# The norms' factors by Sqrt on ScalarE and reciprocal on VectorE, in a two-block transformer kernel on one core

## The reference

```
def rmsnorm(x, g):
    xf = x.astype(jnp.float32)
    y = xf * lax.rsqrt(jnp.mean(xf * xf, axis=-1, keepdims=True) + EPS)
    return (y * g.astype(jnp.float32)).astype(x.dtype)

# a layer of the first stack
h = modulate(x, g_pre_mix[l], sh_m, sc_m)          # rmsnorm(x, g) * (1 + scale) + shift
x = x + gt_m * rmsnorm(mixer(h), g_post_mix[l])
h = modulate(x, g_pre_ffn[l], sh_f, sc_f)
x = x + gt_f * rmsnorm(swiglu(h), g_post_ffn[l])

# a layer of the second stack
x = x + mixer_2(rmsnorm_2(x, norm_mix))
x = x + swiglu_2(rmsnorm_2(x, norm_ffn), w_gate, w_up, w_down)
```

## Time and profile before

| | |
|---|---|
| median of 3 runs | 3402.07 us (3381.19 to 3405.97) |
| the profiled execution | 3400.29 us, of it the span 3398.5 us |
| TensorE busy | 3115.9 us, 92% of the span |
| VectorE busy | 1730.7 us, 51% |
| ScalarE busy | 1104.5 us, 33% |
| GpSimd busy | 1051.5 us, 31% |
| mean granted TensorE clock | 0.951 of full |

### The profile page before, as it was taken

The page is one execution under the profiler, slowest core; times in us unless marked ns, Lnnn a source line. Parts: engine busy times, 40 slices in busy tenths (PEclk is TensorE's granted clock), DMA queues, the critical chain, the costliest instruction groups (busy, mean ns, idle before and its releaser), DMA issues.

```text
span 3398.5 us, 48631 instructions
## 1 busy us (share of the span) xinstructions
PE 3115.9 (92%) x16966; PEld 2498.9 (74%) x16970; DVE 1730.7 (51%) x2899; ACT 1104.5 (33%) x1903; POOL 1051.5 (31%) x573
## 2 busy tenths in 40 slices
PE   6778789999997899899998998899999989899997
PEld 3656668888886766699895765677887866677876
DVE  4655767854335566343345766343333257643423
ACT  3145153021113155432224324352223226543222
POOL 1121123233322311244443420244444311244443
PEclk9879989999998999899999989899999989999999
DMA  6200323443211100222222210222223100022222
GB/s 242 71 1 16 133 78 120 161 135 126 72 56 39 43 1 26 68 84 95 93 84 69 75 44 1 71 94 94 96 91 109 62 25 2 14 94 97 93 93 80
DMA packets 74344, 258.83 MB, mean 76 GB/s; under 512 B 9456, under 2 KB 12016, under 8 KB 72688
## 3 DMA queue, kind: packets, MB, share of 16 engines
q1 hardware_dynamic: 60256, 205.61, 18.2%
q10 hardware_dynamic: 13968, 51.65, 4.5%
HBM read 253.03 MB, written 2.10 MB: 75 GB/s over the span
## 4 chain that ended last, share of the span: by engine, by line
PE 83%; DVE 5%; issue 5%; ACT 3%; DVEq 1%; SPq 1%; POOL 0%; DMA 0%; ACTq 0%; POOLq 0%; PEldq 0%
PE ps L805 57%; PE ps L783 6%; PE ps L2479 2%; PE ps L2493 2%; PE ps L2636 1%; PE ps L417 1%; PE ps L1649 1%; PE ps L1842 1%; PE ps L1078 1%; DVE ps L380 1%; PE ps L2700 1%; PE ps L1654 1%; PE ps L2613 1%; ACT w_hi L625 1%; PE ps L2612 1%
## 5 line engine op out<-in xcount | busy, mean ns | idle before, releaser
L743 POOL TENSOR_TENSOR w_lo<-w_raw,w_hi 128x1024 fp32r<-128x1024 f32 (+1 forms) x373 | 918.8, 2466 | 1862.6 <-ACT w_hi L625 1862.6
L625 ACT ACTIVATE w_hi<-w_raw 128x1024 fp32r<-128x1024 f32 (+1 forms) x373 | 385.7, 1038 | 1217.9 <-PE ps L805 975.1
L805 PE MATMUL ps<-h_hi,w_hi 128*128 128x258 f32 (+2 forms) x1824 | 326.2, 332 | 49.6 <-ACT w_hi L625 45.7
L805 PEld LDWEIGHTS ps<-h_hi,w_hi 128*128 128x128 f32 x1824 | 274.2, 196 | 89.0 <-issue 46.3
L805 PE MATMUL ps<-h_hi,w_lo 128*128 128x258 f32 (+2 forms) x1824 | 308.2, 321 | 0.0
L805 PE MATMUL ps<-h_lo,w_hi 128*128 128x258 f32 (+2 forms) x1824 | 308.2, 321 | 0.0
L805 PEld LDWEIGHTS ps<-h_hi,w_lo 128*128 128x128 f32 x1824 | 265.2, 190 | 27.5
L805 PEld LDWEIGHTS ps<-h_lo,w_hi 128*128 128x128 f32 x1824 | 264.8, 190 | 26.8
L805 PE MATMUL ps<-hb_hi,w_hi 128*128 128x512 f32 x672 | 171.0, 396 | 1.8 <-issue 1.7
L901 DVE CAST act_hi<-f_t 128x512 f32 (+1 forms) x88 | 164.0, 1863 | 12.6
L805 PE MATMUL ps<-hb_hi,w_lo 128*128 128x512 f32 x672 | 169.8, 394 | 0.0
(11 more groups left out here) (345 smaller groups left out, 5181.6 us busy)
## 6 DMA issues: line engine op xcount, KB each, us to landing
w_raw<-in_ffn_in SPq DMA_DIRECT2D x176, 512.0 KB, 3.4
mod_row<-in_w_mod_rows ACTq DMA_DIRECT2D x80, 512.0 KB, 4.3
w_raw<-in_ffn_out SPq DMA_DIRECT2D x64, 512.0 KB, 3.4
w_raw<-in_ev_in SPq DMA_DIRECT2D x26, 512.0 KB, 3.4
w_raw<-in_ffn_out SPq DMA_DIRECT2D x32, 384.0 KB, 3.0
w_raw<-in_od_in SPq DMA_DIRECT2D x21, 512.0 KB, 3.4
mod_ring<-in_w_mod SPq DMA_DIRECT2D x8, 1024.0 KB, 13.1
w_raw<-in_wo_in SPq DMA_DIRECT2D x12, 512.0 KB, 3.4
```

What stands on the lines that cost most here:

```text
L625: act.activation(k.w_hi[:, s, 0:self.KT * P], k.w_raw[:, s, 0:self.KT * P], ACT.Copy).then_inc(k.sems["w_hi_ready"], 1)
L743: ins = pool.tensor_tensor(k.w_lo[:, s, 0:self.KT * P], k.w_raw[:, s, 0:self.KT * P], k.w_hi[:, s, 0:self.KT * P].bitcast(F32), ALU.subtract)
L805: ins = pe.matmul(k.ps[:, self.step * s + g, 0:t1 - t0], w[:, s, c * P:(c + 1) * P], h[:, c, t0:t1], start=(n == 0), stop=(n == len(parts) ...
```

## The change

`inverse_root` becomes `root`, one activation `Sqrt` with the epsilon as bias, and VectorE takes the reciprocal in place, behind a new semaphore at each of the fourteen places (`y_root`, `root_ready`, `ckv_root`). VectorE's waits for the finished factor stay where they are. The small activations of the epsilon at L450 and L502 become `Sqrt` as well. No DMA changes.

```
-def inverse_root(act, chain, k, out, mean):
-    chain.link(act.activation(out, mean, ACT.Ln, bias=k.eps[:, 0:1]))
-    return act.activation(out, out, ACT.Exp, scale=-0.5)
+def root(act, k, out, mean):
+    return act.activation(out, mean, ACT.Sqrt, bias=k.eps[:, 0:1])

 class Pre:
     def act_factor(self, act, chain):
         k, T = self.kit, self.T
         act.wait_ge(k.sems["mean_ready"], self.b["mean_ready"] + 1)
-        inverse_root(act, chain, k, k.n_r[:, :T], flat(k.ps[:, 4:6])[:, :T]).then_inc(k.sems["r_ready"], 1)
+        root(act, k, k.n_r[:, :T], flat(k.ps[:, 4:6])[:, :T]).then_inc(k.sems["root_ready"], 1)
+
+    def dve_factor(self, dve):
+        k, T = self.kit, self.T
+        dve.wait_ge(k.sems["root_ready"], self.b["root_ready"] + 1)
+        dve.reciprocal(k.n_r[:, :T], k.n_r[:, :T]).then_inc(k.sems["r_ready"], 1)

 class Modulation, vector:
         modulated(k, dve, 0, "scale_mix", (0, 1)).then_inc(k.sems["mod_done"], 1)
+        self.pre.dve_factor(dve)
         dve.wait_ge(k.sems["mod_done"], 1)
         self.pre.dve_shift(dve)

 class Gate, scalar:
-        act.activation(k.ln_eps[:], k.eps[:], ACT.Ln)
+        act.activation(k.ln_eps[:], k.eps[:], ACT.Sqrt)
...
-        inverse_root(act, chain, k, r, r).then_inc(k.sems["y_rstd"], 1)
+        root(act, k, r, r).then_inc(k.sems["y_root"], 1)
 class Gate, vector (the same in Norm):
+        dve.wait_ge(k.sems["y_root"], b["y_root"] + 1)
+        dve.reciprocal(r[:, :T], r[:, :T]).then_inc(k.sems["y_rstd"], 1)
         dve.wait_ge(k.sems["y_rstd"], b["y_rstd"] + 1)
...
         self.pre.dve_lo(dve, DC - 1)
+        self.pre.dve_factor(dve)

 class Linear, vector:
         if self.norm:
+            if self.prev and isinstance(self.prev, Linear) and self.prev.post is self.norm:
+                self.norm.dve_factor(dve)
             dve.wait_ge(k.sems["r_ready"], self.norm.b["r_ready"] + 1)

 class LatentBeside, scalar at m == 11, vector at m == 10:
-            inverse_root(act, chain, k, k.ps[:, 4, :], k.ps[:, 4, :]).then_inc(S["ckv_r"], 1)
+            root(act, k, k.ps[:, 4, :], k.ps[:, 4, :]).then_inc(S["ckv_root"], 1)
...
+            dve.wait_ge(*self.count2("ckv_root", 1))
+            dve.reciprocal(k.ps[:, 4, :], k.ps[:, 4, :]).then_inc(S["ckv_r"], 1)
             dve.wait_ge(*self.count2("ckv_r", 1))
```

More of the change, by code:

```diff
@@ L185, in __init__ @@
         self.T = groups[-1][1]
-        self.b = {n: kit.reserve(n, c) for n, c in (("pre_hi", DC), ("pre_lo", DC), ("mean_ready", 1), ("r_ready", 1))}
+        self.b = {n: kit.reserve(n, c) for n, c in (("pre_hi", DC), ("pre_lo", DC), ("mean_ready", 1), ("root_ready", 1), ("r_ready", 1))}
     def act_shift(self, act, chain):
@@ L434, in __init__ @@
         kit.stages[-2].feed()
-        self.b = {n: kit.reserve(n, c) for n, c in (("y_mean", 1), ("y_rstd", 1), ("gate_t", DC), ("gate_x", DC), ("sq_ready", DC), ("sq_used", DC - 1))}
+        self.b = {n: kit.reserve(n, c) for n, c in (("y_mean", 1), ("y_root", 1), ("y_rstd", 1), ("gate_t", DC), ("gate_x", DC), ("sq_ready", DC), ("sq_used", DC - 1))}
         self.pre = Pre(kit, norm_cols, shift, groups, hi, lo)
@@ L493, in __init__ @@
         kit.stages[-2].feed()
-        self.b = {n: kit.reserve(n, 1) for n in ("y_mean", "y_rstd")}
+        self.b = {n: kit.reserve(n, 1) for n in ("y_mean", "y_root", "y_rstd")}
     def tensor(self, pe):
@@ L1304, in __init__ @@
             ("iw_turned", 1), ("iw_in", 1), ("idx_mm", self.PAIRS), ("idx_relu", self.PAIRS), ("idx_acc", self.PAIRS),
-            ("ckv_sq", 1), ("ckv_mean", 1), ("ckv_r", 1), ("ckv_n", 1), ("ckv_turned", 1), ("ckv_tok", 1),
+            ("ckv_sq", 1), ("ckv_mean", 1), ("ckv_root", 1), ("ckv_r", 1), ("ckv_n", 1), ("ckv_turned", 1), ("ckv_tok", 1),
             ("lat_mm", 4), ("lat_in", 4), ("vb_turned", 4), ("vb_in", 4), ("lam_dots", 1), ("lam_exp", 1))}
```

## The result

The changed kernel takes 3417.98 us, the median of 13 runs (3411.54 to 3430.81); the kernel before took 3402.07, the median of 13 beside them (3381.19 to 3412.84). The difference of the two medians is 15.9 us. The ratio of the runs, which is not that of the two medians, is 1.0076, with a 95% interval of [1.0057, 1.0096]: 19 to 33 us slower. The forecast was +24, as a time 3424 us, in a range of 3405 to 3441. The profiled execution took 3428.48 us, of it the span 3426.7, that is 28.2 us more span than before.

A forecast was written before the change was run, and what follows sets the result against it. The prediction took TensorE, carrying 83% of the chain of waits, as the bound, so other engines' changes count only where it stands still. Its terms sum to +24.2 us on 3400.3, giving 3424 us, range 3405 to 3441.

The forecast's parts named there:

- four branch norms, to TensorE's first product: Branch norms in Gate: Sqrt and reciprocal outlast Ln, load and Exp; +5.8 us with 768 tokens, +3.0 with 512.
- four ends of `Gate`: Factors at the end of Gate: the stage ends with VectorE's reciprocal, ScalarE waiting; +5.8 us with 768 tokens, +3.0 with 512.
- last norm: The last norm: the 512-token branch norm's chain once more, with nothing beside it; +1.5 us.
- latent's norm: The latent's norm: the reciprocal enters VectorE's own queue and delays TensorE's turning; +1.75 us.
- three behind a `Linear`: Three factors behind a Linear: the later factor is covered by TensorE's second-slab products; 0, uncovered 1.3 us each.
- first stage: First stage: ScalarE's copy of the modulation's products starts earlier without load and Exp; -1.0 us.
- window attention's load: Window attention: its first Exp needs a table load after Sqrt, where it needed none; +1.3 us.
- TensorE's clock: Four ends of Gate: longer waits mean more half-rate time, sites at 472 and 1836 joining 1429's pattern; +3 us of 0 to 6.
- the dearer: Rival on exposed long rows: the reciprocal costs 8.5 ns a column, +14 us, together +38, 3438 us; chance 0.14.
- the faster reciprocal: Rival on exposed long rows: about 1 ns a column, so the kernel is not slower, -10 us, 3390; chance 0.06.
- rival in which clock and window attention cost up to 12 us more: Half clock lasts 6 us longer at each Gate, or the load falls into every attention turn; 3436 us; chance 0.08.
- rival in which less is exposed: Table switches worth their drain, or part of TensorE's wait being another's; +8 to +13 us, 3411; chance 0.12.

The follow-up runs named there:

- recip60: The changed kernel with each of the fourteen reciprocals over 60 columns only, into a scratch row, and Sqrt's scale 0 (factor a constant): 3387.84 us, ratio 0.9962 to the kernel before.
- recip3: The changed kernel with every reciprocal taken three times in place: 3529.77 us, ratio 1.0391 to the kernel before.
- lnexp_one_set: The kernel before, with one table set holding both Ln and Exp loaded by name ahead of each wait for a mean: 3383.40 us, ratio 0.9947.
- the second measurement: The changed kernel run once more, unchanged, beside the kernel before: 3427.17 us, ratio 1.0080.
- late: The changed kernel with the reciprocal at the end of Gate moved behind the meeting, into the next Linear: 3423.95 us, ratio 1.0062 to the kernel before.

## Why the prediction was right

| step | predicted | measured in the traces |
|---|---|---|
| four branch norms, to TensorE's first product | +5.8, +3.0 | +5.8, +2.3 |
| four ends of `Gate` | +5.8, +3.0 | +5.6, +2.9 |
| last norm | +1.5 | +1.5 |
| latent's norm | +1.75 | +1.55 |
| three behind a `Linear` | 0 | 0 |
| first stage | -1.0 | -1.25 |
| window attention's load | +1.3 | +1.3 (TensorE's wait 1.06 to 2.33) |
| TensorE's clock | +3 | +1.8 |
| sum | +24.2 | +21.5 |

The interval that begins with Sqrt is 428.87 to 434.85, 5.98 us, for a predicted 5.99, and 4.17 for 4.18 with 512 tokens. The last norm goes from 2.68 to 4.17. What carried the forecast is that the reciprocal's price per column came from the same operation. The rivals of the dearer and of the faster reciprocal both fall with its groups in the profile after, and recip60 and recip3 show from both sides that these rows, and nothing else of the change, make the loss. The rival in which clock and window attention cost up to 12 us more falls with the 1.8 and 1.3 of the table. The rival in which less is exposed was right in kind and small here: behind the branch norms with 512 tokens GpSimd's low parts cover 0.4 us each, which the prediction, going by what ended TensorE's wait, had at nothing. With a faster factor the same cover takes far more, as recip60 and lnexp_one_set show.

The clock was the weakest term, and its 1.8 is a sum of unlike things; that it comes near the 3 is luck. The 32 products behind the first, the second and the third wait (at the second with two turning products ahead of them) took 7.15, 9.43 and 6.61 us before and take 8.13, 8.35 and 5.73; at the fourth the two turning products and the 16 behind them went from 4.69 to 7.50. The site at 1836 did go to half clock as predicted, the one at 472 lost 1 us, and the other two won 2 back.

The traced terms make +21.5, the rest of the span +18.6 and +17.0 in two profiles, the medians +16 and +25, the two ratios +26 and +27. Of the 3 to 4.5 us between the terms and the rest, 2.5 are the stretch of 256.6 us in the one profile of the kernel before. The median of 3417.98 is 6 below the forecast; the second measurement's is 3 above it, and runs of one kernel spread over 20 us, so neither distance says anything of the terms.

lnexp_one_set shows that between `Ln` and `Exp` a load costs its own 1.28 us and nothing more. The Trainium skill (ScalarE: Activation LUTs, What ACT_TABLE_LOAD costs) adds a drain to every switch, by which the sum would have been an estimated +12. The trace has 6.25 ns a column up to 768 columns. By the repeat count of 8 that the Trainium skill gives (VectorE: DVE Perf Modes, First, the fixed hardware budget) the sum would have been an estimated +37.

Two things in the prediction were incomplete, and neither moved the sum. The prediction had ScalarE wait at the meeting for the reciprocal, but priced the ends of `Gate` by the reciprocal's length alone; late shows that 5.5 of the 8.5 us by which the four waits grew come from where it stands, ahead of the meeting, with ScalarE's load and rounding behind it instead of beside it. And 1% as what the measurement tells from no change was too coarse for 13 runs of each kernel: the interval is 13 us wide, and it tells +0.8% from no change.

## What to carry to other kernels

Before an elementwise function is moved from ScalarE to VectorE, take its price per column from the widest row of that very operation: the reciprocal's 3.35 us for 512 columns are about five times VectorE's plain product (0.69), and more than an activation and a table load together (0.58 and 1.28). When two functions alternate on ScalarE, see whether one set holds both and ask for it by name where ScalarE is idle, behind the engines' meeting: here that gained 13 to 16 us of the rest of the span, where replacing both functions lost 17 to 19. Follow a factor to the engine that bounds the kernel before its time is counted as gained or lost, since what stands between them can be held by a third engine. And when two profiles differ, subtract first the stretches that hold nothing of the change: here they were worth 10 us of 28 in one pair and 6 of 19 in another.

## What the runs showed of the hardware

- TensorE's clock in two attention stages is not the same from kernel to kernel, though their instructions are: 26.0, 29.9 or 35.7 us for one and 239.5 to 257.6 for the other. Behind one wait it was 0.66 or 1.00, depending on what TensorE did in the wait (3.79 us or 2.18 for sixteen products).
- Some of VectorE's operations are stretched beside GpSimd's product of 128x1024, and some are not. Stretched: two `TENSOR_SCALAR` from 0.75 to 2.73 us, the one at 1929.63 from 0.43 (before the change, with GpSimd idle) to 2.33, and the addition `x<-x,n_t` of 512 columns from 0.69 to 2.34. Not stretched: the reciprocal, 4.95 us with GpSimd's product beside it and without, and the product at 2242.73 that reads PSUM, 0.69 us with GpSimd at work from 2242.23 to 2244.63.
- A table load ahead of a meeting of the engines is not free although ScalarE is idle afterwards: 0.6 to 0.8 us of 1.28 did not come back there, GpSimd's first cast waiting 0.6 longer for ScalarE; behind the meeting the whole 1.28 came back.
